# Key/value projection from un-normed input, its norm applied to the product; the next projection's input written during it; operand rounding moved ahead of an exponential in attention

## The reference, cut to what matters

```python
x = x + gated_deltanet_mixer(rms_norm(x, a_norm[i]), ...)        # layer A
def shared_kv(x, kv_norm, w_kv, k_gain):
    kv = rms_norm(x, kv_norm) @ w_kv                             # 1024 -> 512
    k, v = jnp.split(kv, 2, axis=-1)
    k = rms_norm(k.reshape(B, T, B_KV_HEADS, B_HD), k_gain)      # 4 heads of 64
    ...
def swa_sink_mixer(h, w_in, q_gain, ...):                        # h = rms_norm(x, b_norm)
    q, z = jnp.split(h @ w_in, 2, axis=-1)                       # 1024 -> 2048 + 2048
    q = rms_norm(q.reshape(B, T, B_Q_HEADS, B_HD), q_gain) * (B_HD ** -0.5)
    ...                                                          # scores, bias, softmax with sink, values
    return (o * jax.nn.silu(z)) @ w_out
```

## Time and profile before

| what | us |
|---|---|
| median of 3 runs | 2824.14 |
| the three runs | 2812.67 to 2825.64 |
| the profiled execution, time | 2829.67 |
| the profiled execution, span | 2828.0 |
| PE busy in it | 2695.8 (95%) |
| DVE, ACT, POOL busy in it | 1625.2, 1000.6, 378.7 |

### The profile page before, as it was taken

The page is one execution under the profiler, slowest core; times in us unless marked ns, Lnnn a source line. Parts: engine busy times, 40 slices in busy tenths (PEclk is TensorE's granted clock), DMA queues, the critical chain, the costliest instruction groups (busy, mean ns, idle before and its releaser), DMA issues.

```text
span 2828.0 us, 38623 instructions
## 1 busy us (share of the span) xinstructions
PE 2695.8 (95%) x14601; PEld 2185.5 (77%) x14601; DVE 1625.2 (57%) x2360; ACT 1000.6 (35%) x1412; POOL 378.7 (13%) x275
## 2 busy tenths in 40 slices
PE   7999999889999989999999999999999996999998
PEld 5787787666777758888888888888887775888886
DVE  5665656465666664544544444654445897744455
ACT  4544435336565643222342222322223212422222
POOL 1100001002000011111121111211110441211110
PEclk9999999889999989999979999999999996999998
DMA  3221212012222212223213222232322110232221
GB/s 115 87 82 55 90 61 90 32 45 83 70 84 69 69 50 98 94 99 102 92 45 99 95 96 97 91 103 89 104 89 89 60 59 9 82 104 94 99 89 59
DMA packets 167801, 227.35 MB, mean 80 GB/s; under 512 B 5361, under 2 KB 148219, under 8 KB 167699
## 3 DMA queue, kind: packets, MB, share of 16 engines
q1 hardware_dynamic: 163523, 217.23, 23.5%
q0 software_dynamic: 2368, 8.47, 0.9%
q10 hardware_dynamic: 1808, 0.21, 0.1%
HBM read 223.71 MB, written 2.18 MB: 80 GB/s over the span
## 4 chain that ended last, share of the span: by engine, by line
PE 82%; DVE 9%; issue 5%; ACT 3%; DVEq 0%; DMA 0%; POOL 0%; ACTq 0%; SPq 0%; POOLq 0%
PE ps L376 19%; PE ps L378 19%; PE ps L377 19%; PE ps L760 4%; PE ps L762 4%; PE ps L761 4%; DVE w_lo L357 2%; DVE dw_y L2076 1%; DVE probs L1597 1%; PE ps L1467 1%; PE ps L366 1%; PE ps L367 1%; PE ps L368 1%; PE ps L1478 1%; PE ps L1449 1%
## 5 line engine op out<-in xcount | busy, mean ns | idle before, releaser
L352 ACT ACTIVATE w_hi<-w_raw 128x2048 fp32r<-128x2048 f32 x203 | 388.4, 1913 | 918.8 <-PE ps L378 909.9
L376 PE MATMUL ps<-h_hi,w_hi 128*128 128x512 f32 x1472 | 573.8, 390 | 4.7 <-DVE glu L2045 3.6
L378 PE MATMUL ps<-h_hi,w_lo 128*128 128x512 f32 x1472 | 572.8, 389 | 0.0
L377 PE MATMUL ps<-h_lo,w_hi 128*128 128x512 f32 x1472 | 572.6, 389 | 0.0
L357 DVE TENSOR_TENSOR w_lo<-w_raw,w_hi 128x2048 fp32r<-128x2048 f32 x203 | 471.8, 2324 | 121.3 <-ACT w_hi L352 121.3
L376 PE MATMUL ps<-a_hi,w_hi 128*128 128x512 f32 x1024 | 403.1, 394 | 26.2 <-issue 15.2
L421 DVE SCALAR_TENSOR_TENSOR xT<-ps,xT 128x512 f32<-128x512 f32 x504 | 337.1, 686 | 158.0 <-PE ps L378 156.7
L377 PE MATMUL ps<-a_lo,w_hi 128*128 128x512 f32 x1024 | 401.5, 392 | 0.0
L378 PE MATMUL ps<-a_hi,w_lo 128*128 128x512 f32 x1024 | 401.2, 392 | 0.0
L1681 POOL TENSOR_TENSOR f_gate<-f_gate,n_rstd 128x512 f32<-128x512 f32 x88 | 176.8, 2011 | 1123.6 <-ACT f_gate L1675 1123.6
L376 PEld LDWEIGHTS ps<-h_hi,w_hi 128*128 128x128 f32 x1472 | 276.3, 188 | 63.0 <-DVE glu L2045 4.5
(11 more groups left out here) (334 smaller groups left out, 3049.0 us busy)
## 6 DMA issues: line engine op xcount, KB each, us to landing
w_raw<-in_ffn_w_in_dram SPq DMA_DIRECT2D x88, 1024.0 KB, 5.1
w_raw<-in_ffn_w_out_dram SPq DMA_DIRECT2D x44, 1024.0 KB, 4.9
w_raw<-in_a_w_in_dram SPq DMA_DIRECT2D x24, 1024.0 KB, 5.4
w_raw<-in_b_w_in_dram SPq DMA_DIRECT2D x16, 1024.0 KB, 5.4
w_raw<-in_conv_w_pw_dram SPq DMA_DIRECT2D x12, 1024.0 KB, 5.3
w_raw<-in_a_w_out_dram SPq DMA_DIRECT2D x8, 1024.0 KB, 5.0
w_raw<-in_b_w_out_dram SPq DMA_DIRECT2D x8, 1024.0 KB, 5.0
bias_cur<-rel_scratch POOLq DMA_DIRECT2D x8, 512.0 KB, 3.9
```

What stands on the lines that cost most here:

```text
L352: nc.scalar.activation(w_hi[:, t % 2], w_raw[:, t % 2], ACT.Copy).then_inc(hi_done, 1)
L376: nc.tensor.matmul(dst, wh, xh, start=(k == 0), stop=False)
L377: nc.tensor.matmul(dst, wh, xl, start=False, stop=False)
L378: m = nc.tensor.matmul(dst, wl, xh, start=False, stop=last)
```

## The change

Four things are edited. (1) The key/value input is `xT` times the gain only; `act_gained` and `dve_gained` write it while the last O tile of layer A is added, the squares are summed on POOL (`gp_sums`) instead of DVE, and the sum over channels, the turn of the norm and the keys' sums of squares are placed between chunks of the two projection tiles on PE. The product is multiplied by `n_rstd` when DVE takes it out of PSUM (`taken`, formerly a copy on ACT). (2) `dve_h` writes the attention input behind T_KV+1: chunk n as soon as T_KV+1 has read chunk n (`kv_h_read`), and the last one when the tile is done. (3) The squares of the first queries are summed before the keys are reversed, in banks 4 and 5, and `k_cur`, `v_cur` are written ahead of the gate (`act_group`), in the first round and in the loop. (4) In attention, ACT rounds `a_hi` between Ln and Exp, and DVE's scaling of the queries stands behind `a_lo`.

```diff
-        def arriving(pe, h_from, wh, wl, banks):
+        def arriving(pe, h_from, wh, wl, banks, read=None, behind={}):
...
                     if k == KC - 1:
                         ins.then_inc(chunk_done, 1)
+                    elif c == 1 and read is not None:
+                        ins.then_inc(read, 1)
+                if k in behind:
+                    behind[k]()
...
         def dve_h(dve, m, q, gain, prev_tile=None):
...
-            if prev_tile is not None:
-                wait_chunk(dve, prev_tile, 1)
             for n in range(KC + 1):
                 if n < KC:
                     if n >= 2:
                         dve.wait_ge(h_ready, 8 * q + n - 1)
+                    if prev_tile is not None:
+                        if n < KC - 1:
+                            dve.wait_ge(kv_h_read, n + 1)
+                        else:
+                            wait_chunk(dve, prev_tile, 1)
...
-                        pe.wait_ge(in_free, in_before(u) + IN_CREDIT)
+                        pe.wait_ge(in_free, in_before(u) + IN_CREDIT - 2)
                         arriving(pe, h_from, wh, wl, (0, 1))
...
-            add_chunks(dve, t + 1, range(0, 8), r, period, stat=1 if last else None)
+            if last:
+                split_tile(dve, T_KV)
+                dve_gained(dve, 1, gain_of("kv_norm"), lambda n: add_chunks(dve, t + 1, (n,), r, period))
...
         def pe_kv(pe):
-            pe_tile(pe, T_KV, h_from=8)
-            pe_tile(pe, T_KV + 1)
-            out_all_free(pe, T_KV)
...
+            pe_tile(pe, T_KV, h_from=8, behind={6: lambda: pe_sums(pe, 1, T_KV)})
...
+            pe_tile(pe, T_KV + 1, h_from=8, read=kv_h_read, behind={0: lambda: pe_spread(pe, 1), 4: key_sums})
...
                 kv_pe.done(name, ins)
+            pe_q_squares(pe, -1, 1, 4)
             fill(4)
...
             kv_dve.wait(pe, "vr")
-            pe_q_squares(pe, -1, 1)
             fill()
...
         def act_kv(act):
-            round_tile(act, T_KV + 1)
-            for c in range(4):
-                wait_chunk(act, T_KV + c // 2, c % 2)
-                fn(kvf[:, c], ps[:, c], ACT.Copy).then_inc(in_free, 1)
...
-            act_q_root(act, -1, 1)
-            round_tile(act, T_B + 2)
+            kv_dve.wait(act, "vr")
+            kv_act.wait(act, "kr0")
+            act_group(act, 0)
             for c in range(2):
                 act_z_take(act, c, T_B + 1, None, 1)
...
+            def taken(c):
+                wait_chunk(dve, T_KV + c // 2, c % 2)
+                v.tensor_tensor(kvf[:, c], ps[:, c], n_rstd[:], ALU.mult).then_inc(in_free, 1)
+
+            taken(0)
+            taken(1)
+            split_tile(dve, T_B)
+            dve_h(dve, 1, 2, gain_of("b_norm"), prev_tile=T_KV + 1)
...
             copy(3)
-            if not last:
-                act_q_root(act, j, pp)
+            def operand():
+                for c in range(2):
+                    b_dve.wait(act, f"gt{c}{pp}", j)
+                    fn(a_hi[:, pp, c], zb_gate[:, pp, c], ACT.Copy).then_inc(a_hi_ready, 1)
+
+            if last:
+                operand()
+            else:
+                act_q_root(act, j, pp, meanwhile=operand)
                 act_z_take(act, 0, t + 1, j, pp)
-            for c in range(2):
-                b_dve.wait(act, f"gt{c}{pp}", j)
-                fn(a_hi[:, pp, c], zb_gate[:, pp, c], ACT.Copy).then_inc(a_hi_ready, 1)
-            if not last:
+                if pp == 1:
+                    act_group(act, j + 1)
                 act_z_take(act, 1, t + 1, j, pp)
...
             if not last:
                 split_tile(dve, t + 2, j, NB)
-                dve_q_scale(dve, j, pp)
...
             dve_pair(dve, t_out, zb_gate[:, pp], i, NB)
+            if not last:
+                dve_q_scale(dve, j, pp)
...
             gp_a(pool, A_PAIRS - 1)
+            gp_sums(pool, 1)
             pool.wait_ge(rel_stored, 16)
...
-            act_squares(act, 1, added(T_A_END - 1))
+            act_gained(act, 1, 1, T_A_END - 1, gain_of("kv_norm"))
+            round_tile(act, T_KV + 1)
             act_root(act, 1)
-            act_h(act, 1)
```

More of the change, by code:

```diff
@@ L313, in build @@
         gate_stored, gate_loaded = sem("gate_stored"), sem("gate_loaded")
+        kv_h_read = sem("kv_h_read")
         SMALL = 16 * 5
-        FIRST_TILE = {1: T_KV, 6: T_PW1}
+        FIRST_TILE = {6: T_PW1}
         LN_STAT = 7
@@ L379, in products, with pe_tile @@
             return m
-        def pe_tile(pe, t, i=None, period=0, h_from=None, all_free=False, between=None):
+        def pe_tile(pe, t, i=None, period=0, h_from=None, all_free=False, between=None, read=None, behind={}):
             kind, slot = TILES[t], t % 2
@@ L389, in pe_tile @@
                 if h_from is not None:
-                    arriving(pe, h_from, wh, wl, (bank, bank + 1))
+                    arriving(pe, h_from, wh, wl, (bank, bank + 1), read, behind)
                     return
@@ L1336, in pe_kv @@
             kv_act.wait(pe, "vt")
+            q_act.wait(pe, "ln11", -1)
             for j in range(B_KV):
@@ L1353, in act_kv, with key_root @@
             fn = nc.scalar.activation
-            round_tile(act, T_KV + 1)
-            for c in range(4):
-                wait_chunk(act, T_KV + c // 2, c % 2)
-                fn(kvf[:, c], ps[:, c], ACT.Copy).then_inc(in_free, 1)
-                if c < 2:
-                    act.wait_ge(in_free, in_before(T_KV) + c + 1 + IN_CREDIT)
-                    kv_act.done(f"sq{c}", fn(kv_sq[:, c], kvf[:, c], ACT.Square))
-            round_tile(act, T_B)
-            kv_pe.wait(act, "ss")
-            kv_act.done("root", fn(tok[:, 0:16], ps[:, 4, 0:16], ACT.Sqrt, bias=eps[:, 0:1], scale=1.0 / B_HD))
-            act_h(act, 2)
+            round_tile(act, T_B)
+            for c in range(2):
+                act.wait_ge(in_free, in_before(T_KV) + c + 1 + IN_CREDIT)
+                kv_act.done(f"sq{c}", fn(kv_sq[:, c], kvf[:, c], ACT.Square))
+            def key_root():
+                kv_pe.wait(act, "ss")
+                kv_act.done("root", fn(tok[:, 0:16], ps[:, 4, 0:16], ACT.Sqrt, bias=eps[:, 0:1], scale=1.0 / B_HD))
+            act_h(act, 2, after={4: key_root})
             round_tile(act, T_B + 1)
             q_act.begin(act, 6)
-            b_act.begin(act)
+            b_act.begin(act, 2)
+            in_all_free(act, T_B)
             for c in range(2):
                 act_q_take(act, c, T_B, None, -1, 1)
+            round_tile(act, T_B + 2)
             kv_pe.wait(act, "vt")
@@ L1394, in dve_kv @@
                     tok[:, 8 * c:8 * c + 8].rearrange("p (n o) -> p n o", o=1).to_broadcast([P, 8, B_HD])))
-            split_tile(dve, T_B)
-            dve_h(dve, 1, 2, gain_of("b_norm"), prev_tile=T_KV + 1)
             split_tile(dve, T_B + 1)
+            taken(2)
+            taken(3)
             for c in range(2):
@@ L1406, in dve_kv @@
                     ps[:, 6:8].rearrange("p k t -> p (k t)").rearrange("p (n d) -> p n d", d=B_HD)))
+            q_dve.begin(dve, 2)
+            b_dve.begin(dve)
+            split_tile(dve, T_B + 2)
+            dve_q_scale(dve, -1, 1)
             kv_pe.wait(dve, "vr")
@@ L1409, in dve_kv @@
                                             ps[:, 6:8].rearrange("p k t -> p (k t)")))
-            q_dve.begin(dve, 2)
-            b_dve.begin(dve)
-            dve_q_scale(dve, -1, 1)
-            split_tile(dve, T_B + 2)
         def width(b):
@@ L1423, in last_step, with pe_q_squares @@
             return isinstance(j, int) and 2 * j + pp == B_STEPS - 1
-        def pe_q_squares(pe, j, pp):
+        def pe_q_squares(pe, j, pp, bank=2):
             b_dve.wait(pe, f"add3{pp}", j)
@@ L1428, in pe_q_squares @@
                 q_act.wait(pe, f"sq{c}{pp}", j)
-                q_pe.done(f"ss{c}{pp}", nc.tensor.matmul(ps[:, 2 + c], head_ones[:], q_sq[:, c], start=True, stop=True))
+                q_pe.done(f"ss{c}{pp}", nc.tensor.matmul(ps[:, bank + c], head_ones[:], q_sq[:, c], start=True, stop=True))
         def pe_b(pe, j, pp):
@@ L1442, in scores @@
                         q_dve.before(pe, "nq11", j)
-                    b_act.wait(pe, "vc0", j)
+                    b_act.before(pe, "vc1", j)
                 else:
@@ L1524, in act_q_root, with act_group @@
                 q_act.done(f"rq{c}{pp}", nc.scalar.activation(q_sq[:, c], q_sq[:, c], ACT.Exp, scale=-0.5))
+        def act_group(act, j):
+            if not isinstance(j, int) or j:
+                b_pe.wait(act, "pv31", j - 1)
+            b_act.done("kc1", nc.scalar.activation(
+                k_cur[:], k_rev[:, bass.ds(j, 1), :].rearrange("p o t -> p (o t)"), ACT.Copy))
+            b_act.done("vc1", nc.scalar.activation(
+                v_cur[:], v_rev[:, :, bass.ds(j, 1), :].rearrange("p q o d -> p q (o d)"), ACT.Copy))
         def act_b(act, j, pp):
@@ L1530, in act_b @@
             m = lambda name, ins: b_act.done(f"{name}{pp}", ins)
-            if pp == 0:
```

(6 more changed lines are left out.)

30 lines of the change are left out of this document (19 added, 11 removed).

## The result

The changed kernel takes 2790.74 us, the median of 5 runs (2789.56 to 2796.64), against 2822.99 before (5 runs, 2812.67 to 2825.64). The ratio is 0.9889, with a 95% interval of 0.9867 to 0.9910: 32.3 us, or 1.1%, faster. The forecast was 31.1 us less and 2793.0.

The account below looks back on a forecast made before the run. PE, busy for 95% of the span, was taken as the bound. Gains of 22.9 + 2.6 + 5.6 = 31.1 us from the median 2824.14 gave 2793.0, with a range of 2783 to 2806.

Parts of the forecast that it names:

- Key/value stage: From layer A's last O tile to the first attention scores: 59.0 us against 81.9, so 22.9 gained.
- The wait of 1.0 at the queries' squares: Behind the transposes, PE waits for a mark DVE gives during its second copy of the keys: 1.0 us (bounds 0 and 1.8).
- The wait of 0.3 for POOL: Ahead of the sum over channels, PE waits 0.3 us for POOL's last sum (bounds 0 and 8.0).
- the small groups: Small matmuls of the key/value stage: sums and turn 1.6 us, keys' sums 1.7.
- the 3.00 of the earlier trace: Duration of POOL's last sum where attention ends in the profile before, against 1.62 each for sums 2 to 6.
- the forecast's 14.1 for seven rounds: If POOL's sums and DVE's `h_lo` excluded each other wholly: rounds of 1.27 + 0.74, a wait of 1.1, 30.3 gained.
- First half-step: First half-step of attention: without the idle before it, it looks like the second, 2.6 us gained (bounds 0 and 2.6).
- Seven gaps: PE's gaps at attention's O tiles go with rounding ahead of Exp: 0.8 us each, 5.6 gained (bounds 0 and 6.2).
- What pays for it: In attention, Exp comes about 1.8 us later and DVE's scaling ends near 705.8 instead of 704.0, hidden with 1.9 to spare.
- rival (d): Slower than before: late scaling of queries makes PE wait for banks in each of seven half-steps; chance 0.02.
- Rival (c): Waits move instead of going: T_B waits 5 us, the scores still 5.5; gain 20.6, 2803.5 us; chance 0.06.
- Rival (e): No change: PE's clock falls for want of pauses, so the work stretches; chance 0.01.

Follow-up runs that it names:

- e8_pool_double: The changed kernel with an unused addition of the same size ahead of each of POOL's seven sums; 2792.72 us in one run.
- parts 1 to 3 alone: The changed kernel with part (4), the attention part, undone; median 2793.05 us, ratio 0.9886, and 2798.81 us, ratio 0.9906, when run again.
- e4_input_after_tile: The changed kernel with the attention input written only when T_KV+1 has been multiplied, as before; median 2789.80 us, ratio 0.9881.
- e6_group_late: The changed kernel with `k_cur`, `v_cur` written behind the gate again, in the first round and in the loop; 2789.80 us in one run.
- e9_both_late: The changed kernel with both the first queries' squares behind the reversal and `k_cur`, `v_cur` behind the gate again; 2787.93 us in one run.
- e5_squares_late: The changed kernel with the first queries' squares, their Ln and Exp, and DVE's scaling behind the keys' reversal again; 2790.33 us in one run.

## Why the forecast was right, and which terms were off

**Key/value stage: 59.0 forecast, 58.03 measured.** Its parts, from PE's timeline: E to T_B's start 25.49 (forecast 2 x 10.9 + 3.3 + 0.3 = 25.4), T_B 10.89 (10.9), the turn 21.65 (21.7 and a wait of 1.0). Two terms were mis-sized. *The wait of 1.0 at the queries' squares did not occur.* The mark (`b_dve.begin`, an increment that stands on DVE's queue by itself) is the one that POOL's transfer waits for too. In the earlier trace rows it stood behind one copy and came 0.72 after that copy's start; I took it to come as far into the second copy, where it stands behind two. But after, the transfer starts 0.74 after the first of the two copies, before the second has begun, and PE's squares start 0.67 after it, right behind the transposes (1.91 long with the tail of the last). *The wait of 0.3 for POOL did not occur*: its last sum ended at E + 8.75, a quarter us ahead of my window of E + 9.0 to E + 10.9. Against them, the small groups took 3.69 instead of 3.3.

Why the seventh sum did not take the 3.00 of the earlier trace rows, and what a round costs, is seen in single rows of POOL and DVE (after, three in a row, then before, the row that ran beside the 3.00):

```profile
583.21 1.56 POOL L589 TENSOR_TENSOR n_sum<-n_sum,n_sq 128x512 f32<-128x512 f32 x1
584.14 1.18 DVE L578 SCALAR_TENSOR_TENSOR h_lo<-xT,cols,h_hi 128x512 fp32r<-128x512 f32 x1
584.91 1.57 POOL L589 TENSOR_TENSOR n_sum<-n_sum,n_sq 128x512 f32<-128x512 f32 x1
```

```profile
1055.29 2.28 DVE L357 TENSOR_TENSOR w_lo<-w_raw,w_hi 128x2048 fp32r<-128x2048 f32 x1
```

The `h_lo` starts during one sum and ends 0.55 after it (584.77, 585.32); the next sum starts during that `h_lo` and ends 1.16 after it (586.48). The rounds that follow repeat this to a hundredth: the two take turns, at 0.55 + 1.15 = 1.70 a round. The 3.00 was such a turn too: that sum began 0.42 after DVE's split of a weight tile and ended at 1058.71, 1.14 after the split (1057.57). After the change no split stood ahead of the seventh sum, which took 1.56; the split that followed it was the one to wait, 2.77 instead of 2.28. So the 3.00 belongs to the split beside it and not to POOL. `e8_pool_double` has the same again: the last of POOL's added operations, begun 0.05 behind a split of 2.29, took 3.13, where others of them took 1.04. (The two `h_lo` that the forecast put at 1.44 each in the earlier trace rows took 1.17 and 1.79.) The Trainium skill's rule on the shared ports of VectorE and GpSimd (page "SBUF — State Buffer", section "SBUF: two separate sides") says that the one that comes second is blocked for the whole of the other's instruction, and the trace agrees in that the two take turns; that the ports are the reason is the page's word, not the rows'. What made the forecast's 14.1 for seven rounds too large against 11.94 measured, from the first sum's start to the last one's end, is the price of a round: 1.27 + 0.74 = 2.01 are two recorded durations, and the turns cost 1.70.

**First half-step: 2.6 forecast, 2.27 measured** (before against parts 1 to 3 alone). The idle ahead of it was the reason: before, PE did its first scores behind the wait of 5.5 at the lower level of the clock, until about 672:

```profile
669.00:671.00 2.00, 2.00 (x5) 1.61 (x6) 1.81 (x12) 0.00 (x0) 1.85 (x6) 0.50 0.93 348
```

**Seven gaps: 5.6 forecast, about 7.4 measured.** The mechanism held, the size did not: 0.8 each was the idle time of the trace with nothing added. The second O tile now starts 36.18 after the last matmul of the first, where it was 37.13: 0.95 for the gap; another 0.14 lies between the O tile's start and the next scores (10.97 against 11.11). The trace counts idle time from the modelled end of a 0.39 matmul, while the next can start 0.23 after its start, so a gap costs 0.16 more than its figure. The remaining 0.14 was seen in each run and its cause is open; the first matmul behind a gap takes 0.49 instead of 0.39.

**What pays for it** came out as placed: Exp starts at 674.80, the scaling ends at 676.88, the first add to `xT` at 678.57 does not wait for it. No O tile waits for banks, so rival (d) has no trace. Rival (c): T_B and the scores wait for nothing; had the input stayed behind the tile, there would have been a wait of 2.3 at T_B and a stretch longer by 4.75 (`e4_input_after_tile`). Rival (e): the clock of the windows reads 1.00.

**The sum.** 24.1 + 2.27 + 7.4 = 33.8, less 1.16 in the last half-step, make the 32.65 of the stretch; the forecast's 31.1 had two waits too many (1.3) and seven gaps too small (1.8), and in the other direction 0.4 too little for the small groups and 0.3 too much for the first half-step. None of these takes the total near an end of the range. The medians say 32.3. The mechanisms held; that the total agrees this well with a median is partly luck, since runs of one kernel lie 15 us apart in one set and 19 in another.

## What to carry to other kernels

Where one engine is busy for 95% of the span, sum up its idle gaps in one stretch, and add what it loses at the lower clock behind each long one: a wait of 8.0 cost about 11. A gap's price is the distance between starts, not the idle figure. When an operation is moved ahead on one engine, look at what stands ahead of its successor on the next one: here the rounding ahead of Exp gains only if the scaling that waits for Exp leaves its place too. And where two engines take turns, a long instruction that starts first on one makes the other's short one look slow: look beside a slow row before its duration is used as a price.

## What the runs showed of the hardware that was not expected

**The clock behind a pause.** Behind pauses of PE of 1.5 in `e6_group_late` the window reads 1.00 (2.4 GHz), behind one of 2.3 in `e4_input_after_tile` it reads 0.50 (1.2 GHz), and behind the 3.7 of `e9_both_late` as well, where the next half-step is 1.34 longer than with the change. Not all of the 1.34 is the clock: in `e6_group_late`, where it stays at 1.00, the half-step is 0.54 longer too. The three, in this order:

```profile
643.00:645.00 2.00, 2.00 (x14) 1.58 (x11) 1.42 (x10) 0.82 (x1) 1.85 (x4) 1.00 0.00 0
```

```profile
605.00:606.00 1.00, 1.00 (x4) 0.81 (x3) 0.96 (x3) 0.63 (x1) 0.00 (x0) 0.50 0.00 0
```

```profile
641.00:643.00 2.00, 2.00 (x6) 1.52 (x6) 1.42 (x12) 0.81 (x4) 0.00 (x0) 0.50 0.00 0
```

**The same code at several speeds.** In the last half-step, where PE is busy for only 70% of the time, three kernels with the same work there took 44.30, 45.46 and 41.80. The slice of it that comes fourth of six, in the profiles of before, after and `e5_squares_late`:

```profile
1027.90:1035.28 7.38, 5.85 (x24) 3.27 (x24) 2.64 (x6) 0.60 (x1) 0.00 (x0) 0.50 0.00 0
```

```profile
992.02:999.60 7.58, 4.96 (x24) 3.01 (x24) 3.68 (x7) 1.34 (x4) 0.00 (x0) 0.70 0.01 3
```

```profile
989.47:996.44 6.97, 3.38 (x26) 2.00 (x24) 4.20 (x8) 1.91 (x4) 0.00 (x0) 1.00 0.00 1
```

The clock was granted at 0.50, 0.70 and 1.00 for the same work. Over the whole last half-step it is 0.69, 0.74 and 0.84: the shortest has the highest clock, but the longest, after, has not the lowest, so the clock does not account for the 1.16. Layer A, with its many short matmuls, varies as well: between 480 and 540 us the clock was 1.00 where it ended at 578.72, and 0.89 where it ended at 588.32. What decides it in an execution, I could not tell from the traces. The 1.16 lost in the last half-step lies inside the spread of the kernels that keep parts (1) to (3) wholly or in the main (41.80 to 45.93), so no run shows it as a cost of the change; that it is none is not shown either.

**A mark overtakes the copies ahead of it.** DVE's increment that stands behind two copies in the program had released POOL's transfer 0.74 after the start of the first (transfer at 625.58, copy at 624.84, the pair 2.35 long), with the second copy not yet begun. So such a mark, an increment that stands by itself and not on an instruction, did not say here that the work ahead of it was done.
